# FFN output of a diffusion layer on one core: who issues the residual loads, the broadcast rows and the result stores

## The reference, cut to what matters

```python
h2 = _rmsnorm(x, p['norm2_g']) * (1 + sc2) + sh2
gu = h2 @ p['w_ffn_in']
gt, up = gu[..., :FFN_HIDDEN], gu[..., FFN_HIDDEN:]
x = x + g2 * ((jax.nn.silu(gt) * up) @ p['w_ffn_out'])
...
y_prompt = _rmsnorm(xp, final_g)
y_sample = _rmsnorm(xs, final_g)
```

## Time and profile before

| | us |
|---|---|
| median of 3 runs | 2475.3 (2471.97 to 2478.43) |
| the profiled execution, own time | 2476.16 |
| its span, first to last instruction | 2474.4 |
| PE busy | 2363.6 (96%) |
| DVE busy | 1184.0 (48%) |
| ACT busy | 782.5 (32%) |
| POOL busy | 155.9 (6%) |

### The profile page before, as it was taken

How to read it: one execution, slowest core, us unless ns; L and a number is a source line. 1 busy time by engine, 2 the same in 40 slices (tenths; PEclk the granted TensorE clock), 3 DMA queues, 4 the chain that set the end, 5 groups by cost and what they waited for, 6 DMA issues and landing times. The chain is left out here.

```text
span 2474.4 us, 44030 instructions
## 1 busy us (share of the span) xinstructions
PE 2363.6 (96%) x17899; PEld 2179.3 (88%) x17899; DVE 1184.0 (48%) x1912; ACT 782.5 (32%) x1284; POOL 155.9 (6%) x193
## 2 busy tenths in 40 slices
PE   7999999999999999989999999989999999898987
PEld 5887789999999899889999998779999999877866
DVE  5231111004544677645555457676555665435344
ACT  5311111113342223234444543243223232233333
POOL 0000000001100011012111010010000000000000
PEclk9999999999999999999999999999999999999999
DMA  6335522225453433123002094322212221355553
GB/s 267 120 114 180 178 108 99 83 83 184 163 179 105 149 115 107 65 104 105 17 17 85 14 343 144 113 68 81 76 57 79 79 78 55 102 181 198 175 191 130
DMA packets 120564, 296.31 MB, mean 120 GB/s; under 512 B 15440, under 2 KB 67360, under 8 KB 111088
## 3 DMA queue, kind: packets, MB, share of 16 engines
q1 hardware_dynamic: 84928, 228.44, 27.0%
q10 hardware_dynamic: 31536, 50.74, 5.5%
q0 software_dynamic: 3968, 15.21, 1.6%
HBM read 219.89 MB, written 74.52 MB: 119 GB/s over the span
## 5 line engine op out<-in xcount | busy, mean ns | idle before, releaser
L60 PE MATMUL ps<-mergedr,wt 128*128 128x512 f32 x1188 | 279.6, 398 | 34.6 <-DVE wt L2919 34.6
L60 PEld LDWEIGHTS ps<-mergedr,wt 128*128 128x128 f32 x1188 | 229.1, 193 | 84.9 <-DVE wt L2919 36.5
L60 PE MATMUL ps<-h_hi,fill_whi 128*128 128x384 f32 x672 | 235.3, 350 | 4.0 <-PEq L80 3.4
L60 PE MATMUL ps<-h_lo,fill_whi 128*128 128x384 f32 x672 | 226.3, 337 | 2.4 <-issue 2.4
L60 PE MATMUL ps<-h_hi,fill_wlo 128*128 128x384 f32 x672 | 226.4, 337 | 0.0
L60 PE MATMUL ps<-ys,mergedr 128*128 128x256 f32 (+1 forms) x1056 | 219.1, 296 | 0.9 <-DVE xb L2766 0.4
L60 PEld LDWEIGHTS ps<-ys,mergedr 128*128 128x128 f32 x1056 | 173.9, 190 | 1.3 <-issue 1.3
L60 PE MATMUL ps<-prj_whi,h_hi 128*128 128x512 f32 (+1 forms) x432 | 164.9, 382 | 4.1 <-DVE h_lo L624 4.1
L2917 DVE TENSOR_TENSOR mergedr<-wraw,mergedr 128x1024 fp32r<-128x1024 f32 x66 | 80.9, 1225 | 170.5 <-ACT mergedr L2606 169.7
L60 PE MATMUL ps<-prj_wlo,h_hi 128*128 128x512 f32 (+1 forms) x432 | 161.8, 375 | 0.0
L60 PE MATMUL ps<-prj_whi,h_lo 128*128 128x512 f32 (+1 forms) x432 | 161.8, 374 | 0.0
(11 more groups left out here) (397 smaller groups left out, 4778.3 us busy)
## 6 DMA issues: line engine op xcount, KB each, us to landing
wraw<-in_w_ffn_out SPq DMA_DIRECT2D x66, 512.0 KB, 3.5
wraw<-in_w_ffn_in SPq DMA_DIRECT2D x22, 1024.0 KB, 5.0
prj_raw<-in_w_ada SPq DMA_DIRECT2D x16, 1024.0 KB, 5.9
fill_raw<-in_w_fill SPq DMA_DIRECT2D x30, 512.0 KB, 4.5
bg_dram<-fill_st ACTq DMA_DIRECT2D x72, 192.0 KB, 2.0
xf<-bg_dram POOLq DMA_DIRECT2D x24, 576.0 KB, 7.4
wraw<-a_dram SPq DMA_DIRECT2D x66, 192.0 KB, 3.5
tok_dram<-prj_tst ACTq DMA_DIRECT2D x45, 256.0 KB, 2.0
```

The costliest lines, as they stand in the source:

```text
L60: mm = pe.matmul(out, lhs[a], rhs[b], start=first and n == 0, stop=last and n == 2, skip_group_check=onto)
```

## The change

The three broadcast rows, the nine residual loads and the nine result stores leave SyncE's stream and go into GpSimd's. SyncE's stream in the FFN output is then operands alone. GpSimd waits for the end of the FFN input's products and for the stores of `x1`, issues the first three residual loads and, behind them, the three broadcast rows; then in each of the nine rounds of the last norm it takes the power, loads the residual of the tile three further on when VectorE has added this one, and after every third round stores three results. The wait of SyncE for the last stores of `a` moves from ahead of operand 2 to behind operand 5 of stage 0. Nothing is computed otherwise, and no size changes.

```diff
-            sp.wait_ge(mm, 14 * NH)
-            sp.dma_start(g2, g.gate_rows[1, D:2 * D].partition_broadcast(P)).then_inc(c_in, 16)
-            sp.dma_start(g2p, g.gate_rows[0, D:2 * D].partition_broadcast(P)).then_inc(c_in, 16)
-            sp.dma_start(fg, io["final_g"].partition_broadcast(P)).then_inc(c_in, 16)
-            for s in range(2):
-                sp.wait_ge(x_out[s], 32 * (5 - s))
-                sp.wait_ge(a_out[s], 32 * (NH // 2))
...
-            residuals(0)
             for t in range(3):
                 for j in range(2 if t == 0 else 0, 6):
                     operands(NH * t + j, j % 2, j, t)
-                if t:
-                    for i in range(3 * t - 3, 3 * t):
-                        put_y(i)
-                    residuals(t)
+                if t == 0:
+                    for s in range(2):
+                        sp.wait_ge(a_out[s], 32 * (NH // 2))
                 with sp.Fori(0, 8) as i:
                     for e in range(2):
                         operands(2 * i + NH * t + 6 + e, e, 2 * i + 6 + e, t)
-            for i in (6, 7, 8):
-                put_y(i)
-            for n in range(3):
-                sp.wait_ge(y_out[n], 48)
 
         @block.gpsimd
...
+            gp.wait_ge(mm, 14 * NH)
+            for s in range(2):
+                gp.wait_ge(x_out[s], 32 * (5 - s))
+            for n in range(3):
+                gp.dma_start(res[n], g.x1_dram[n * P:n * P + P, :]).then_inc(r_in, 16)
+            gp.dma_start(g2, g.gate_rows[1, D:2 * D].partition_broadcast(P)).then_inc(c_in, 16)
+            gp.dma_start(g2p, g.gate_rows[0, D:2 * D].partition_broadcast(P)).then_inc(c_in, 16)
+            gp.dma_start(fg, io["final_g"].partition_broadcast(P)).then_inc(c_in, 16)
...
             for i in range(NT):
                 gp.wait_ge(mean_done, i + 1)
                 gp.tensor_tensor(rstd[:, i:i + 1], ms[:, i:i + 1], half[:], ALU.pow).then_inc(y_rstd, 1)
+                if i < 6:
+                    gp.wait_ge(added, i + 1)
+                    gp.dma_start(res[i % 3], g.x1_dram[(i + 3) * P:(i + 4) * P, :]).then_inc(r_in, 16)
+                if i % 3 == 2:
+                    for n in range(i - 2, i + 1):
+                        put_y(n)
+            for n in range(3):
+                gp.wait_ge(y_out[n], 48)
```

More of the change, by code:

```diff
@@ L2386, in _ @@
             store_a(L, 1, 1)
-            sp.wait_ge(mm, 14 * NH)
-            sp.dma_start(g2, g.gate_rows[1, D:2 * D].partition_broadcast(P)).then_inc(c_in, 16)
-            sp.dma_start(g2p, g.gate_rows[0, D:2 * D].partition_broadcast(P)).then_inc(c_in, 16)
-            sp.dma_start(fg, io["final_g"].partition_broadcast(P)).then_inc(c_in, 16)
-            for s in range(2):
-                sp.wait_ge(x_out[s], 32 * (5 - s))
-                sp.wait_ge(a_out[s], 32 * (NH // 2))
-            def residuals(t):
-                for n in range(3):
-                    i = 3 * t + n
-                    if t:
[L2399 to L2405, removed]
-            residuals(0)
             for t in range(3):
@@ L2442, in _, with put_y @@
                     gp.tensor_tensor(s4_first, s4_first, s2[1].bitcast(F32), ALU.subtract).then_inc(s4_done, 1)
+            gp.wait_ge(mm, 14 * NH)
[6 more added lines that the diff above has]
+            gp.dma_start(fg, io["final_g"].partition_broadcast(P)).then_inc(c_in, 16)
+            def put_y(i):
+                gp.wait_ge(y_done, i + 1)
+                dst = g.outs["y_sample"][i * P - P:i * P, :] if i else g.outs["y_prompt"]
+                gp.dma_start(dst, y[i % 3]).then_inc(y_out[i % 3], 16)
             for i in range(NT):
```

## The result

The changed kernel takes 2460.0 us (median of 4 runs, 2458.0 to 2461.9) against 2475.8 of the kernel before beside it: a ratio of 0.9937, 95% interval 0.992 to 0.9955, so 15.8 us or 0.6% faster. The forecast was 2447 with a range of 2440 to 2458. The direction was right, and a little over half of the gain came.

What follows compares the result with a forecast made beforehand. TensorE, busy 96% of the span, was taken as the bound, its gaps due to SyncE's queue. Stages 1 and 2 -24.4, stage 0 -5.6, end +1.9 sum to -28.1 us: median 2447 us, range 2440 to 2458.

Steps and rivals of the forecast that it cites:

- The bound and the reason for the gaps: FFN output: TensorE bounds; three gaps, 29.5 us together, come from late operands held back in SyncE's queue.
- Part 1, stages 1 and 2: Operand 6 no longer waits behind results and residuals; both gaps and their half clock go, -24.4 us.
- the landing of an operand: Stages 1 and 2: an operand sharing the engines evenly with GpSimd's transfers lands in about 5.2 us.
- The slack: Stages 1 and 2: VectorE finishes operand 5 1.2 us early, so a landing up to 6.2 us costs nothing.
- Rival 1: Stages 1 and 2: shared engines make operands land in 9.7 us, 3.5 us gaps plus half clock; 2460 us, chance 0.13.
- Part 2, stage 0: Operand 2 issued 3.9 us earlier; TensorE's gap shrinks to 5.6 us, the clock loss stays: -5.6 us.
- VectorE waits for the rows: Stage 0: VectorE waits for all three broadcast rows, landed at 2163.7, before splitting operand 2; TensorE resumes at 2165.5.
- Rival 2: Stage 0: the wait for broadcast rows replaces the gap, so nothing is gained there; 2453 us, chance 0.16.
- Part 3, the end: End: GpSimd's last three stores go out later and land at 2474.8, +1.9 us, bounds 0 and +5.
- Rival 3: Stage 0: VectorE starves GpSimd's queue, broadcast rows land at 2213, TensorE stands 55 us; 2497 us, chance 0.03.
- rival 4: Whole kernel: nothing moves, the late operand being due to its own traffic; within 1 us of before, chance 0.02.
- The range: Whole kernel: 2440 to 2458 us, from the forecast's bounds with 1 us of scatter, rival 2 and its slow tail.

Runs made afterwards that it cites:

- everything by SyncE: Kernel before, GpSimd issuing nothing: SyncE issues each transfer singly behind later operands, VectorE's wait for the broadcast rows in stage 1; median 2440.2 us, ratio 0.9863.
- stage 0 undone: Changed kernel, but SyncE again waits for the stores and issues the three broadcast rows and first three residual loads ahead of operand 2; 2466.5 us, single run.
- stage 0 late: Changed kernel, but GpSimd's first six transfers are issued singly from operand 4 of stage 0 on, VectorE's wait for the rows in stage 1; median 2456.6 us.
- the end by SyncE: Changed kernel, but SyncE issues the last three result stores as each norm ends and waits for them; median 2457.7 us.
- the two with everything by GpSimd: Changed kernel, GpSimd's transfers spread, first six late, last stores by SyncE; spread transfers released by VectorE's low part (2446.6 us) or ScalarE's high part (2441.2 us).

## Why the prediction was wrong, point by point

- **The bound and the reason for the gaps** were read right. SyncE's queue held the operands back: the gaps of stages 1 and 2 shrank when the transfers left it, and were gone when SyncE issued the same transfers at later places.
- **Part 1, stages 1 and 2, is the step that failed.** It gave -24.4 us. Measured are 6.33 + 6.54 of gap and 6.0 - 1.7 of clock, -17.2: 7.2 us short, 5.5 of it gap and 1.7 clock. The failed step is the landing of an operand, "about 5.2 us", worked out from even sharing with as many bytes of GpSimd's as it has itself. Operand 6 landed in 7.62 us in stage 1 and in 8.34 in stage 2, because it met a load and three stores of 512 KB each. Against the slack as the prediction has it, 6.2 us, that alone makes gaps of 1.4 and 2.1 us.
- **The slack was counted wrong as well**, and gives most of the rest. "A landing of up to 6.2 us costs nothing" holds for one late operand. The loads of one buffer form a cycle: issue, landing, ScalarE, VectorE, next issue. In stage 1 of the changed kernel the cycle of operand 4, from 2262.45, took 9.25 us with a landing of 5.89, so operand 6 went out 1.1 us late; its own cycle, from 2271.70 to VectorE's end at 2282.74, took 11.04 with 7.62. Besides the landing either took 3.4 us. Two units are 8.17 us, so from one cycle to the next only a landing of some 4.8 us is free; the 1.2 us ahead of TensorE are there once. The two cycles took 20.3 us where 16.3 were to be had, 4.0 too many, 1.2 of them covered: 2.8 against a gap of 2.46. In stage 2 the same sum, with cycles of 8.74 and 11.74 us, gives 2.9 against 3.05. The estimate of 5.2 us was already above 4.8.
- **Rival 1 ended at the measured time (2460) by luck**, and only half by its mechanism. Operands did land later than 6.2 us beside GpSimd's traffic, as it has it. But it had gaps of 3.5 us and half clocks in both stages, 13 us in all; they were 2.46 and 3.05 and one half clock, 7.2 us, and no operand of these stages took its 9.7 us. The rest of the miss of 13 us is the end (3.5) and stage 0 (1.4). The run in which SyncE issues everything has the lowest median, so a second queue was not what was needed. The Trainium skill (DMA: Bandwidth & Descriptors, Issuing engines are not separate DMA queues) has it that starting DMAs from more engines saves only the issuing time, and that all of them run on the same 16 DMA engines. In the first point the measurement differs: the gaps of stages 1 and 2 shrank by 6.33 and 6.54 us, where SyncE had issued three loads in 1.81 us; the rest was its wait for VectorE's norms. In the second the trace agrees: operands landed in 5.9 to 8.3 us beside GpSimd's transfers.
- **Part 2, stage 0**, gave -5.6. The gap shrank by 5.05, and the half clock grew by 0.8: -4.2. The last broadcast row landed 10.0 us after its issue at 2153.51. Counted from the start of unit 0 that is 10.9 us, where 2163.7 had meant 12.2. But the step "VectorE waits for the rows" was wrong: operand 2 landed at 2164.2, 0.7 us after the rows, and the run with that wait moved left the gap at 6.02 us. The size came out nearly right by luck, since two waits nearly coincide. Rival 2 fell with it.
- **Part 3, the end**, gave +1.9 and measured +5.4, beyond its bound of +5. The landing was sized right: 4.0 instead of 2.6 us and 0.3 us of later issue make 1.7, where 1.9 was worked out. (Its 1.5 us until data moves and 0.5 to land stand in no row; in the trace after, the packets of these three stores begin 1.1 us behind the first issue and end 0.3 us ahead of the last landing.) The step that failed is that the sum ended with the landing. It put GpSimd's drain, 3.7 us, at nothing without a reason. The drain stood in the trace of before, 3.39 us, begun ahead of the last norm and hidden.
- **Rival 3 and rival 4** did not occur: GpSimd's issues took 0.53 to 0.57 us beside VectorE's work.
- **The range** was the sum of bounds of the terms; two terms came out above their bounds at once, -17.2 against -20.9 for stages 1 and 2 and +5.4 against +5 for the end.

## What to carry to other kernels

Taking transfers out of a queue that feeds the bottleneck is worth the wait they imposed there, but it lets them run beside the feed: place each one where the feed is idle, released by the event "the operand has landed" and not by the one that releases the next operand; here that took the operands beside a store from 5.6 to 5.8 us down to 3.5 to 4.0. One queue with the right order did as well as two (2440 and 2441 us). When a load, its conversion and the release of its buffer form a cycle, compare the whole cycle with the period, and count a one-time slack once. Before an engine is given the last transfers of a program, look at how long its drain is and what hides it now.

## What was not expected of the hardware

- GpSimd's drain at the end of the block is 3.39 us in the two kernels in whose FFN output GpSimd issues nothing (before, everything by SyncE), and 4.85 us in the three where it issues 18 transfers there but not the last stores; in all five it starts with the last power. Behind a wait for its own last stores it is 3.73 us with 21 transfers issued and 3.24 with 15 (stage 0 undone). So each transfer issued goes with about 0.08 us more of drain, an estimate from these traces; that those of 18 had long landed speaks against a wait for landings there. With its own last stores in flight it is 5.94 us. What it waits for was not settled.
- A gap of 2.46 us cost no clock, one of 3.05 us 1.7 us, one of 6.09 us 2.5 us. In five traces (stage 0 late, stage 0 undone, the end by SyncE, and the two with everything by GpSimd) the first two units took about 10.05 instead of 8.46 us at half clock with the same 2.12 us idle before them, and the last two took 8.44 to 11.19 us behind the same 2.96 us. So the same short pause costs nothing in one execution and 1.6 us or more in another, which is part of the scatter; ahead of a gap it costs nothing, because the gap shrinks by as much.
- With the engines otherwise free, an operand that started 0.1 us ahead of a 512 KB store of GpSimd's landed in 5.6 to 5.8 us instead of 3.5; ahead of a 512 KB load by as much, in 4.7 to 5.1.
